# One of 32 experts' weights kept in memory of its own, in a two-layer transformer kernel on one Trainium2 core

## The reference, cut to what matters

```
x = x + mixed @ w_out
h = rmsnorm(x, ffn_norm)
route: one of 4 groups per token, then the 2 best of its 8 experts, with weights w
x = x + sum over a token's experts e of
        w[e] * ((silu(h @ w_gate[e]) * (h @ w_up[e])) @ w_down[e])
out = rmsnorm(x, final_norm)
```

## Time and profile before

| what | value |
|---|---|
| runs, median (lowest to highest of 3) | 2140.3 us (2137.91 to 2140.9) |
| the profiled execution, its own time | 2138.09 us |
| its span in the trace | 2136.3 us |
| TensorE busy | 1869.6 us (88%) |
| TensorE weight loads busy | 1262.1 us (59%) |
| VectorE busy | 715.4 us (33%) |
| ScalarE busy | 319.5 us (15%) |
| read from HBM | 391.68 MB, mean 184 GB/s |
| expert loads | 96 of 2048 KB, median 26.5 us (arena) and 25.9 us (ring) from issue to landing |

### The profile page before, as it was taken

The page is one execution under the profiler, slowest core; times in us unless marked ns, Lnnn a source line. Parts: engine busy times, 40 slices in busy tenths (PEclk is TensorE's granted clock), DMA queues, the critical chain, the costliest instruction groups (busy, mean ns, idle before and its releaser), DMA issues. The chain is left out here.

```text
span 2136.3 us, 31349 instructions
## 1 busy us (share of the span) xinstructions
PE 1869.6 (88%) x13516; PEld 1262.1 (59%) x13516; DVE 715.4 (33%) x1573; ACT 319.5 (15%) x725; POOL 0.2 (0%) x4
## 2 busy tenths in 40 slices
PE   7999997999998996999889999899999867666765
PEld 4465643444443444666568888768878755555554
DVE  1355534333333113333444431356533311111111
ACT  0233303000000002221111100301240100000001
POOL 0000000000000000000000000000000000000000
PEclk9999997999999997999989999899999988888887
DMA  9256651222221200211123444222215899999997
GB/s 407 95 235 259 243 152 40 79 79 79 79 93 54 108 30 30 70 65 65 57 86 150 157 187 168 101 106 90 99 54 222 329 428 428 429 428 428 428 429 309
DMA packets 27646, 393.89 MB, mean 184 GB/s; under 512 B 3248, under 2 KB 4272, under 8 KB 4656
## 3 DMA queue, kind: packets, MB, share of 16 engines
q1 hardware_dynamic: 26960, 388.49, 44.9%
q10 hardware_dynamic: 608, 4.25, 0.9%
HBM read 391.68 MB, written 1.05 MB: 184 GB/s over the span
## 5 line engine op out<-in xcount | busy, mean ns | idle before, releaser
L385 PE MATMUL bank<-layer_input,ring 128*128 128x256 f32 (+1 forms) x2368 | 739.5, 474 | 30.6 <-DVEq L170 17.1
L385 PEld LDWEIGHTS bank<-layer_input,ring 128*128 128x128 f32 x2368 | 459.1, 195 | 301.7 <-issue 235.2
L385 PE MATMUL bank<-arena,ring 128*128 128x256 f32 (+1 forms) x1024 | 304.2, 458 | 12.7 <-ACTq L170 10.5
L385 PEld LDWEIGHTS bank<-arena,ring 128*128 128x128 f32 x1024 | 196.0, 192 | 117.7 <-issue 86.2
L1203 DVE TENSOR_SCALAR arena<-bank,vectors 128x512 f32<-128x512 f32 (+1 forms) x88 | 55.5, 673 | 279.4 <-PE bank L385 279.4
L2439 PE MATMUL bank<-ring,arena 128*32 128x128 f32 x2048 | 85.9, 337 | 61.8 <-DMA ring<-w_moe 61.2
L2439 PEld LDWEIGHTS bank<-ring,arena 128*32 128x32 f32 x2048 | 72.8, 136 | 75.9 <-DMA ring<-w_moe 72.3
L535 DVE TENSOR_SCALAR arena<-bank,ada 128x256 f32<-128x256 f32 x48 | 21.8, 481 | 256.5 <-PE bank L385 256.5
L1207 DVE SCALAR_TENSOR_TENSOR arena<-bank,vectors,arena 128x510 f32<-128x510 f32 (+1 forms) x176 | 100.3, 611 | 13.7 <-DVE arena L1203 7.6
L2439 PE MATMUL bank<-arena 128*32 128x128 f32 x2048 | 72.8, 302 | 33.7 <-DMA arena<-w_moe 32.9
L385 PE MATMUL bank<-arena 128*128 128x128 f32 (+3 forms) x464 | 95.7, 356 | 1.9 <-DVE arena L2428 1.0
(11 more groups left out here) (367 smaller groups left out, 1626.7 us busy)
## 6 DMA issues: line engine op xcount, KB each, us to landing
arena<-w_moe SPq DMA_DIRECT2D x48, 2048.0 KB, 26.5
ring<-w_moe SPq DMA_DIRECT2D x48, 2048.0 KB, 25.9
ring<-w_ffn_in SPq DMA_DIRECT2D x22, 2048.0 KB, 7.6
ring<-w_ada_late SPq DMA_DIRECT2D x16, 2560.0 KB, 10.2
ring<-w_ffn_out SPq DMA_DIRECT2D x8, 2816.0 KB, 9.9
ring<-w_proj SPq DMA_DIRECT2D x7, 3072.0 KB, 10.0
ring<-w_na_pair SPq DMA_DIRECT2D x8, 1536.0 KB, 6.3
ring<-w_ada SPq DMA_DIRECT2D x2, 2048.0 KB, 10.2
```

What stands on the lines that cost most here:

```text
L385: last = pe.matmul(out, a, b, start=(k == 0), stop=(k == len(lhs) - 1))
```

## The change

Expert 28 (`RESIDENT`), the first of the last quad, gets a place of its own, in four pieces: its gate in the whole of `A`; the first half of its up part in the context columns (0 to 255 of each tile) of `H`, eight pieces of 256 columns per partition; the other half in 2048 columns of `arena` below the router's scratch; its down part in the constants, from the table `mean` on. For that the four tables that router and experts read move ahead of `mean` in the constants, the constants' tensor becomes 48 columns wider (4644 instead of 4596), and the router's scratch is 960 columns instead of 1024.

SP issues the down part and both halves of the up part right behind expert 0's three loads. It issues the gate ahead of the loop over the experts, after a new wait on `var_ready` for the fourth group of transposes. The loop ends with expert 27. Experts 29, 30 and 31 go to slots 0, 1 and 0, and wait for the parts of experts 26, 27 and 29. On TensorE the last quad takes expert 28 from the kept place, after a wait for all four of its loads, and the other three from the slots. Both kernels load the same bytes, and the instructions on TensorE, VectorE and ScalarE are the same in number and kind.

```diff
-CONSTS = [("ident", P), ("ones", P), ("mean", P), ("rot_mla", P), ("swap_mla", P), ("cos_mla", LAT), ("sin_mla", LAT),
+CONSTS = [("ident", P), ("ones", P), ("slot", SLOTS), ("before", P), ("ahead", P), ("first4", GROUPS), ("mean", P), ("rot_mla", P), ("swap_mla", P), ("cos_mla", LAT), ("sin_mla", LAT),
           ("rot_nsa", P), ("cos_nsa", LAT), ("sin_nsa", LAT), ("na_mask", LAT),
           ("nsa_mask", 416), ("cmp_keep", 32), ("level_mask", (len(LEVELS) + 1) * P), ("scan_keep", LAT),
-          ("cmp_fold", 16), ("spread", 4 * P), ("first4", GROUPS), ("ahead", P), ("before", P), ("slot", SLOTS)]
+          ("cmp_fold", 16), ("spread", 4 * P)]
...
+KEPT = COFF["mean"][0]
...
+RESIDENT = EXPERTS - QUAD
...
-            self.C = sb("constants", [P, NCONST])
+            self.C = sb("constants", [P, max(NCONST, KEPT + KT * FE)])
...
-        sp.dma_start(self.C[:, :], self.const_d).then_inc(self.rest_in, 16)
+        sp.dma_start(self.C[:, 0:NCONST], self.const_d).then_inc(self.rest_in, 16)
...
         sp.wait_ge(self.phase_done, self.merged)
         for part in range(3):
             load(0, 0, part)
+        w, kept = self.W["moe"][RESIDENT], self.kept_weights()
+        sp.dma_start(kept["down"], w[:, UPS:]).then_inc(self.sem("kept_in"), 16)
+        sp.dma_start(kept["up0"], w[:, UPS // 2:UPS // 2 + 2048].rearrange("p (k t) -> p k t", t=CTX))\
+            .then_inc(self.sem("kept_in"), 16)
+        sp.dma_start(kept["up1"], w[:, UPS // 2 + 2048:UPS]).then_inc(self.sem("kept_in"), 16)
 
...
         sp.wait_ge(self.sem("y_ready"), RESIDUAL_BASE["w_out"] + 4)
@@ -369,11 +376,37 @@
         for part in range(3):
             if part != first:
                 load(1, 1, part)
-        with sp.Fori(0, EXPERTS // 2 - 1) as it:
+        sp.wait_ge(self.sem("var_ready"), self.tail["norms"] + self.TURNED + 3)
+        sp.dma_start(kept["gate"], w[:, 0:UPS // 2]).then_inc(self.sem("kept_in"), 16)
+        parts_used = [self.sem(n) for n in ("moe_gate_done", "moe_up_done", "moe_down_done")]
+        with sp.Fori(0, RESIDENT // 2 - 1) as it:
             for e in range(2):
-                for part, used in enumerate(("moe_gate_done", "moe_up_done", "moe_down_done")):
-                    sp.wait_ge(self.sem(used), it * 2 + e + 1)
+                for part, used in enumerate(parts_used):
+                    sp.wait_ge(used, it * 2 + e + 1)
                     load(it * 2 + e + 2, e, part)
+
+        for x, before in ((RESIDENT + 1, RESIDENT - 2), (RESIDENT + 2, RESIDENT - 1), (RESIDENT + 3, RESIDENT + 1)):
+            for part, used in enumerate(parts_used):
+                sp.wait_ge(used, before + 1)
+                load(x, (x - 1) % 2, part)
...
+    def kept_weights(self):
+
+        return {"gate": self.A[:, :, :].rearrange("p k t -> p (k t)"), "up0": self.H[:, :, 0:CTX],
+                "up1": self.arena[:, FT * T - 960 - 2048:FT * T - 960], "down": self.C[:, KEPT:KEPT + KT * FE]}
+
+    def kept_weight(self, at, n):
+
+        kept = self.kept_weights()
+        if at < UPS // 2:
+            return kept["gate"][:, at:at + n]
+        at -= UPS // 2
+        if at < 2048:
+            return kept["up0"][:, at // CTX, at % CTX:at % CTX + n]
+        if at < UPS // 2:
+            return kept["up1"][:, at - 2048:at - 2048 + n]
+        at -= UPS // 2
+        return kept["down"][:, at:at + n]
...
-        x = self.arena[:, FT * T - 1024:FT * T]
+        x = self.arena[:, FT * T - 960:FT * T]
...
-        assert at + KT * 36 <= 1024
+        assert at + KT * 36 <= 960
...
-        assert at <= FT * T - 1024
+        assert at <= FT * T - 960 - 4 * FE
...
-        def project(x, e):
+        def weight(e, last, at, n):
+            if last and e == 0:
+                return self.kept_weight(at, n)
+            return slots[(e - last) % 2][:, at:at + n]
+
+        def project(x, e, last):
 
             for k in range(KT):
                 for q in range(4):
-                    o = (x * KT + k) * FE + q * P
-                    last = eng.matmul(bank[x][group[q], 0:P], xe[:, k, SLOTS * e:SLOTS * e + SLOTS],
-                                      slots[e % 2][:, o:o + P], start=(k == 0), stop=(k == KT - 1),
-                                      skip_group_check=True)
-            return last
-
-        def down(e):
+                    ins = eng.matmul(bank[x][group[q], 0:P], xe[:, k, SLOTS * e:SLOTS * e + SLOTS],
+                                     weight(e, last, (x * KT + k) * FE + q * P, P), start=(k == 0),
+                                     stop=(k == KT - 1), skip_group_check=True)
+            return ins
+
+        def down(e, last):
 
             for f in range(FET):
                 for g in range(4):
-                    o = UPS + f * D + (g - e) % 4 * 256
-                    last = eng.matmul(bank[2][group[g], 0:256], hidt[:, SLOTS * f:SLOTS * f + SLOTS],
-                                      slots[e % 2][:, o:o + 256], start=(f == 0), stop=(f == FET - 1),
-                                      skip_group_check=True)
-            last.then_inc(s["down_done"], 1)
+                    ins = eng.matmul(bank[2][group[g], 0:256], hidt[:, SLOTS * f:SLOTS * f + SLOTS],
+                                     weight(e, last, UPS + f * D + (g - e) % 4 * 256, 256), start=(f == 0),
+                                     stop=(f == FET - 1), skip_group_check=True)
+            ins.then_inc(s["down_done"], 1)
...
                 for e in range(QUAD):
                     x = x0 + e
-                    gate_in, up_in, down_in = loaded[e % 2]
-                    arrived = i * 32 + 16 * (e // 2 + 1)
+                    gate_in, up_in, down_in = loaded[(e - last) % 2]
+                    arrived = i * 32 + 16 * ((e - last) // 2 + 1)
+                    if last and e == 0:
+                        gate_in = up_in = down_in = self.sem("kept_in")
+                        arrived = 4 * 16
                     eng.wait_ge(gate_in, arrived)
-                    project(0, e).then_inc(s["gate_done"], 1)
+                    project(0, e, last).then_inc(s["gate_done"], 1)
...
                     eng.wait_ge(up_in, arrived)
-                    project(1, e).then_inc(s["up_done"], 1)
+                    project(1, e, last).then_inc(s["up_done"], 1)
...
                     eng.wait_ge(down_in, arrived)
-                    down(e)
+                    down(e, last)
```

## The result

The changed kernel took 2126.42 us (median of 5 runs, 2125.65 to 2127.53) against 2138.17 for the kernel before in 5 runs: a ratio of 0.9944, 95% interval 0.9929 to 0.9958, or 11.8 us with an interval of 9.0 to 15.2. The forecast was 2127.1 us and a gain of 13.2.

A forecast was written before the change was run, and what follows sets the result against it. DMA streaming of expert weights at 428 GB/s was taken as the bound, with idle holes near the router. Holes of 13.46 us less 0.3 for pieces gave 13.2, from 2140.3 to 2127.1 us; range 2122.5 to 2131.5.

The forecast's parts named there:

- Main argument: Expert stage: kept loads fill idle DMA time near the router, so the stream ends earlier by the 13.46 us filled.
- The sum: Whole kernel: 13.46 us of DMA idle time near the router, less 0.3 for small pieces, gives 13.2 us.
- the small pieces: Kept half up part loaded in eight 1 KB pieces per partition: costs 0.3 us, with 0 and 1.0 as ends.
- the first stretch: Sign in the DMA traffic near the router: 1654 to 1662 us should stand at 415 to 428 GB/s.
- the likeliest case: Whole kernel: gains of 11.2 to 14.7 us, so 2125.6 to 2129.1 us.
- the surplus: Kept expert's bytes beyond the idle time near the router: ordinary stream runs 1.24 us late from 1686 us on.
- One issue more: Kept expert's four loads instead of three: cost nothing, at most 0.1 us; a fixed 2 us would leave 11.2.
- The last four experts: Experts 28 to 31: TensorE starts at 2066.7 without waiting; loads still end last, by 9.1 us.
- The slower rival: Last four experts: TensorE at the lower clock becomes the bound beyond 44.2 us; 7.0 us slower, 2147.3; chance 0.05.
- the tail: Behind the last landing: the 14.2 us to the span's end should be unchanged.
- Shared engines: Loads share DMA engines, delaying the output projection's second chunk to about 1658; about 2138.6 us, no change; chance 0.05.
- the whole expert saved: Expert stage: kept loads delay nothing, saving 14.7 us, 2125.6; best case, inside the forecast's bounds given 0.86.

The follow-up runs named there:

- e1: Changed kernel with all four kept-expert loads issued late, behind expert 27's loads; 2139.14 us against 2137.70 for the kernel before, ratio 1.0005.
- e3: Changed kernel with expert 28's weights not loaded at all and TensorE's wait for them gone; ratio to the kernel before 0.9952, stage 477.90 us.
- e5: Changed kernel with the kept down part and half the up part loaded ahead of the output projection's chunks; 2125.83 us, ratio to the kernel before 0.9945.
- e4: Changed kernel with the kept gate also loaded in 1 KB pieces, in two loads; ratio to the kernel before 0.9958, stage 480.90 us.
- e8: The changed kernel itself run again, on the same chip as the others of its call; 2125.19 us, ratio to the kernel before 0.9938.
- e7: Changed kernel with expert 28's gate matmuls done twelve times more on TensorE; ratio to the kernel before 1.0062, stage 502.08 us.
- e9: Changed kernel with expert 28's gate matmuls done five times more on TensorE; ratio to the kernel before 0.9968, stage 485.73 us.
- e2: Changed kernel with only the kept expert's gate load issued late, behind expert 27's loads; ratio to the kernel before 0.9961, stage 482.67 us.
- e6: Changed kernel with expert 28's gate matmuls done three times more on TensorE; ratio to the kernel before 0.9950, stage 479.48 us.
- e10: Kernel of e5 with two extra gate passes filling TensorE's waits in the last expert; ratio to the kernel before 0.9932, stage 479.38 us.

## Why the prediction was right

*Main argument, right.* The gain is the idle time of the DMA engines near the router, filled. e1 shows that the place by itself gives none of it: same place, same order of work, late loads, no gain. e3 and e5 show the upper end, 14.6 and 14.8 us.

*The sum.* 13.46 us of holes. In the changed kernel's stretches there are left 8 x (1 - 402/428) = 0.49, then 0.02, -0.04 and 0.09, together 0.56, so 12.9 filled; the stage shows 12.6. The term that was mis-sized is that of the small pieces, 0.3 taken where e4 shows 0.5. It is also why the first stretch stood at 402 GB/s (395 in e8) and not at the 415 that the forecast had asked for. The remaining 0.3 is less than single profiles differ by, and no row was found for it. The lower end of the likeliest case, 11.2, counts the 0.3 for the pieces twice: 13.46 - 1.0 - 1 is 11.5. That the surplus runs on as a delay was right, with 1.24 forecast and 2.0 - 0.5 = 1.5 measured in e3 without the pieces.

*One issue more, the rule of 2 us.* The Trainium skill (SBUF — State Buffer, The DMA setup-cost knee) names a roughly fixed 2 us for every transfer and puts most of it down to completion latency. Counted in full as time lost in the queue, as the prediction tried it, it would have left a gain of 11.2. The gain was 12.6, and in e4 a fifth load and two MiB of pieces together cost 1.0. In a full queue the 2 us are not seen, as the prediction had it.

*The time.* The stage is 12.6 us shorter, the medians differ by 11.8; the 0.8 between them is less than what executions differ by ahead of the stage. The closeness of 2127.1 to 2126.42 is luck in part: the level of the kernel before, 2140.3 from three runs, was 2.1 us above that of five, 2138.17, and the gain of 13.2 was 1.4 above the medians' 11.8, so that the two errors nearly cancelled. The range had taken such a shift of level in.

*The last four experts.* Expert 28 began at 2069.19, 1.7 us later than forecast after the 0.74 is taken off, since TensorE waited 2.95 us for the up part of 27 and then took 3.19 us for its matmuls instead of 1.95, which was not in the account. It cost nothing. The forecast left TensorE 9.1 us; the waits behind the kept expert sum to 9.2, and e7 and e9 show 8.7 to 9.4 borne. What e7 and e9 measure is by its mechanism another quantity, how late the issue of expert 31's gate load may come before the queue runs empty; here the two are of one size. The slower rival's point of decision was thus well placed. Its condition, the lower clock through four experts, did not come about: expert 28 took 11.1 us in the change's first profile, and only in e9 did its scatter run slowly (5.08 us). The lower clock shows itself in another place, the tail, which the forecast held unchanged: 14.1 and 16.9 us in two executions of the same kernel.

*The other rivals.* Shared engines fell with the landing of 7.6 us for the output projection's chunk; the whole expert saved (2125.6) is what e5 reaches in the stage.

## What to carry to other kernels

In a stage that streams at the rate of its DMA engines, look for the stretches in which the queue is empty and add them up: extra memory is worth the idle time that loads into it can fill, and at most the length of those loads. What is left over can be issued still earlier, before the stage, once its place is dead (2.1 us in the stage in e5, not shown in the time). Memory that only changes where weights lie is worth nothing (e1), and slack on the engine that consumes should be known as a number, since beyond it each us of its delay is a hole in the stream.

## What the runs showed of the hardware

- Loads into 1 KB pieces cost 0.5 us more for each MiB than whole rows, 20% of their time, in a queue that was otherwise full; with 3 MiB in pieces it was 1.0 us more than with 1 MiB (e4).
- The clock granted to TensorE in the tail differs between executions of one kernel, 1.00 and 0.62 in the two profiles of the change; the tail was 14.1 and 16.9 us. In the twelve profiles the last down projection took 1.90 to 1.93 us and the tail 14.0 to 14.2 where TensorE had waited at most 0.96 us for its load (before, change, e1, e2, e6, e10), and 2.43 to 3.58 us and 15.5 to 16.9 where it had waited 1.53 to 2.20 (e3, e4, e5, e7, e8). e9 is the exception, 1.93 us and 14.1 behind a wait of 2.20, after TensorE had worked nearly without a break; so the wait alone does not decide, and the cause is not shown.
- Behind an empty queue the last expert's three loads took 19.3 us from the issue of the first to the start of the last down projection (e7, 2114.25 to 2133.59), 4.6 more than the 14.7 of their bytes.
- Gate matmuls repeated in a straight line on TensorE took 2.5 us a pass instead of 1.85, with idle time on the issue side of up to 2.78 us (e7); the cause was not looked into.
- In e1, with the loads of expert 27 and two kept ones ahead in the queue, the issue of one load held SP for 25.99 us (from 2039.54), while the DMA engines moved 426 to 430 GB/s; a load issued late can thus hold up those behind it. It cost nothing there, and the cause was not looked into.
